# The first gate slot after two norms, computed by token tile instead of after both tiles

## The reference, cut to what matters

```python
        x = x + rms_norm(m, norm_mix_post[layer])
        f = conv_geglu_ffn(rms_norm(x, norm_ffn_pre[layer]), ffn_w_up[layer], ffn_conv_w[layer],
                           ffn_conv_b[layer], ffn_w_down[layer])
...
def conv_geglu_ffn(hn, w_up, conv_w, conv_b, w_down):
    u = depthwise_conv_centered(hn @ w_up, conv_w, conv_b)
    gate, val = jnp.split(u, 2, axis=-1)
    return (jax.nn.gelu(gate, approximate=True) * val) @ w_down
```

## Time and profile before

| | |
|---|---|
| runs | 1027.61, 1025.37, 1022.47 us |
| median | 1025.37 us |
| profiled execution, its own time | 1026.78 us |
| span from first to last instruction | 1024.9 us |
| mean granted TensorE clock (1 is 2.4 GHz) | 0.990 |
| busy: TensorE matmul / weight load | 983.2 us (96%) / 863.7 us (84%) |
| busy: VectorE / ScalarE / GpSimd | 481.9 / 623.3 / 695.9 us |

### The profile page before, as it was taken

The page is one execution under the profiler, slowest core; times in us unless marked ns, Lnnn a source line. Parts: engine busy times, 40 slices in busy tenths (PEclk is TensorE's granted clock), DMA queues, the critical chain, the costliest instruction groups (busy, mean ns, idle before and its releaser), DMA issues. The chain is left out here.

```text
span 1024.9 us, 16075 instructions
## 1 busy us (share of the span) xinstructions
PE 983.2 (96%) x6169; PEld 863.7 (84%) x6169; DVE 481.9 (47%) x993; ACT 623.3 (61%) x1145; POOL 695.9 (68%) x550
## 2 busy tenths in 40 slices
PE   6999998999999898999998899999999998999998
PEld 5898778999999797888877799999977887877786
DVE  3745344444444564777834454444353143223552
ACT  7636557555455785797867564555566568755631
POOL 5977616857577695769678657575778756866663
PEclk9999999999999999999998999999999999999999
DMA  9774325775644564745646455656455845634221
GB/s 334 252 213 156 128 81 175 236 261 170 206 165 138 164 206 126 239 139 198 206 127 222 145 187 183 203 167 205 166 164 174 205 132 180 224 124 159 88 82 42
DMA packets 131946, 178.69 MB, mean 174 GB/s; under 512 B 21457, under 2 KB 94045, under 8 KB 131677
## 3 DMA queue, kind: packets, MB, share of 16 engines
q1 hardware_dynamic: 127693, 169.95, 51.3%
q10 hardware_dynamic: 4176, 7.71, 2.3%
HBM read 176.51 MB, written 5.24 MB: 177 GB/s over the span
## 5 line engine op out<-in xcount | busy, mean ns | idle before, releaser
L519 POOL TENSOR_TENSOR wlo<-raw,whi 128x512 fp32r<-128x512 f32 (+1 forms) x514 | 673.8, 1347 | 297.6 <-ACT whi L1189 281.6
L536 PE MATMUL PS<-Th,whi 128*128 128x256 f32 (+2 forms) x1016 | 290.8, 287 | 3.5 <-DVE Tl L1715 2.8
L537 PE MATMUL PS<-Tl,whi 128*128 128x256 f32 (+2 forms) x1016 | 287.3, 283 | 0.0
L538 PE MATMUL PS<-Th,wlo 128*128 128x256 f32 (+2 forms) x1016 | 287.3, 283 | 0.0
L1189 ACT ACTIVATE whi<-raw 128x1024 fp32r<-128x1024 f32 (+1 forms) x149 | 156.0, 1047 | 165.0 <-PE PS L538 127.9
L533 PE MATMUL PS<-whi,Th 128*128 128x512 f32 (+1 forms) x512 | 204.1, 399 | 7.9 <-DVE Tl L1764 3.3
L1790 DVE SCALAR_TENSOR_TENSOR arena<-PS,cols,arena 128x255 f32<-128x255 f32 (+1 forms) x272 | 118.6, 478 | 192.1 <-ACT arena L1321 165.6
L536 PEld LDWEIGHTS PS<-Th,whi 128*128 128x128 f32 (+2 forms) x1016 | 194.9, 192 | 9.6 <-issue 5.6
L534 PE MATMUL PS<-wlo,Th 128*128 128x512 f32 (+1 forms) x512 | 198.1, 387 | 0.0
L535 PE MATMUL PS<-whi,Tl 128*128 128x512 f32 (+1 forms) x512 | 197.9, 387 | 0.0
L537 PEld LDWEIGHTS PS<-Tl,whi 128*128 128x128 f32 (+2 forms) x1016 | 194.9, 192 | 1.8 <-issue 0.7
(11 more groups left out here) (235 smaller groups left out, 1034.0 us busy)
## 6 DMA issues: line engine op xcount, KB each, us to landing
raw<-in_ffn_w_up_dram SPq DMA_DIRECT2D x44, 1024.0 KB, 5.1
raw<-in_ffn_w_down_dram SPq DMA_DIRECT2D x22, 1024.0 KB, 4.9
raw<-in_w_in_dram SPq DMA_DIRECT2D x22, 1024.0 KB, 5.1
raw<-in_c_w_in_dram SPq DMA_DIRECT2D x16, 1024.0 KB, 5.3
raw<-in_ab_w_in_dram SPq DMA_DIRECT2D x14, 1024.0 KB, 6.6
raw<-in_c_w_out_dram SPq DMA_DIRECT2D x8, 1024.0 KB, 5.8
raw<-in_ab_w_out_dram SPq DMA_DIRECT2D x4, 1024.0 KB, 4.9
raw<-in_c_w_in_dram SPq DMA_DIRECT2D x8, 512.0 KB, 5.4
```

The source lines that it names most:

```text
L519: i = nc.gpsimd.tensor_tensor(wlo[n % NLO][:, c:e], raw[n % NRAW][:, c:e], whi[n % NHI][:, c:e].bitcast(F32), ALU.subtract)
L536: mm(o, wh, ah, start=first, stop=False)
L537: mm(o, wh, al, start=False, stop=False)
L538: return mm(o, wl, ah, start=False, stop=last)
```

## The change

`norm_T` is kept for the very first norm alone, `warm` goes, and `first_gate` takes the first gate slot of both feed-forward parts. It computes the slot by token tile: 128 tokens move in place of 256, so that 96 products of 128 columns replace 48 of 256. Tile 1 is turned after 42 of the 48 products of tile 0. `post_norm` on ScalarE and VectorE takes at boundaries 1 and 3 the order that it had at boundary 4: half of the first value slot is rounded before tile 1's squares, `Th` and `Tl` of tile 0 come between the steps of tile 1, then the other half, the squares of `x`, the whole next gate slot, and `Th` of tile 1.

```diff
-            def warm(bank, n):
-
-                for _ in range(n):
-                    mm(PS[:, bank, :], ident, cst[:, 0:512], start=True, stop=True)
-
-            def norm_T(l):
...
-                    if l and t == 0:
-                        warm(4 - norm_bank(l), 3)
...
+            def first_gate(l):
+
+                s = 2 * l + 1
+                tile_T(s, 0)
+                n = slot_no[("G", l, 0)]
+                pe.wait_ge(*low(n))
+                h, w = whi[n % NHI], wlo[n % NLO]
+                for t in range(NT):
+                    for m in range(2):
+                        for k in range(KD):
+                            if (t, m, k) == (0, 1, 6):
+                                tile_T(s, 1)
+                            if m == 0:
+                                pe.wait_ge(*at("T_lo", (("n", s, t), k)))
+                            c = k * 256 + m * P
+                            i = three(PS[:, 0, m * S + t * P:m * S + (t + 1) * P], h[:, c:c + P], w[:, c:c + P],
+                                      Th[:, k, t * P:(t + 1) * P], Tl[:, k, t * P:(t + 1) * P], k == 0, k == KD - 1, False)
+                i.then_inc(*done("w_used", n))
...
-                        slot_fm(("G", l, i), 2 * (i % 2), ("n", 2 * l + 1) if i == 0 else None)
-                        if i == 0:
-                            pe.wait_ge(*at("T_lo", (("n", 2 * l + 1), KD - 1)))
+                        if i:
+                            slot_fm(("G", l, i), 2 * (i % 2))
+                        else:
+                            first_gate(l)
...
-            norm_T(1)
...
-            norm_T(3)
...
                 if l + 1 == 2:
                     high(n + 2)
-                if l + 1 == 4:
+                else:
                     high_part(n + 2, 0)
                 squares(1, 0)
                 squares(1, 1)
-                if l + 1 in (2, 4):
-                    tile_hi(0, 0, 4)
+                tile_hi(0, 0, 4)
                 root_post(1)
-                if l + 1 in (2, 4):
-                    tile_hi(0, 4)
-                    if l + 1 == 4:
-                        high_part(n + 2, 1)
-                    normed(1)
-                    high(n + 3)
-                    tile_hi(1)
-                    return
+                tile_hi(0, 4)
+                if l + 1 != 2:
+                    high_part(n + 2, 1)
                 normed(1)
-                high(n + 2)
-                T_hi(("n", l + 1), KD, 0, norm_bank(l + 1), lambda k: col(gain, k))
+                high(n + 3)
+                tile_hi(1)
```

More of the change, by code:

```diff
@@ L628, in to_T, with norm_T @@
                     i.then_inc(*done("turned", (name, k)))
-            def warm(bank, n):
-                for _ in range(n):
-                    mm(PS[:, bank, :], ident, cst[:, 0:512], start=True, stop=True)
-            def norm_T(l):
+            def norm_T():
                 for t in range(NT):
-                    if l == 0:
-                        pe.wait_ge(*at("n_hn", (l, t)))
+                    pe.wait_ge(*at("n_hn", (0, t)))
                     for k in range(KD):
-                        if l and k % 4 == 0:
-                            pe.wait_ge(*at("n_hn", (l, t, k // 4)))
-                        i = tr(PS[:, norm_bank(l) + k // 2, (k % 2) * S + t * P:(k % 2) * S + (t + 1) * P],
+                        i = tr(PS[:, norm_bank(0) + k // 2, (k % 2) * S + t * P:(k % 2) * S + (t + 1) * P],
                                hn[:, t, k * P:(k + 1) * P], ident)
                         if t == NT - 1:
-                            i.then_inc(*done("turned", (("n", l), k)))
-                    if l and t == 0:
-                        warm(4 - norm_bank(l), 3)
+                            i.then_inc(*done("turned", (("n", 0), k)))
             def tile_T(l, t):
@@ L740, in _ @@
             tr(PS[:, 0, 0:8], rowm, ident[0:8, 0:8]).then_inc(*done("mix0_T"))
-            norm_T(0)
+            norm_T()
             pe.wait_ge(*at("mix0_col"))
@@ L1740, in product @@
                     return tt(hn[:, t, 512 * hf:512 * hf + 512], PS[:, b0 + 2 * t + hf, :], gpost[:, 512 * hf:512 * hf + 512], ALU.mult)
-                tiles = l + 1 in (2, 4)
                 def post(t):
@@ L1747, in post @@
                     lk(product(t, 1))
-                    if tiles and t:
+                    if t:
                         tile_lo(0, 0, 4)
@@ L1780, in post_norm @@
                     normed(t)
[L1781 to L1784, removed]
+                tile_lo(1)
             def taps(dst, src, ws, shift):
```

## The result

The changed kernel takes **1032.58 us** (median of 20 runs, 1030.64 to 1044.58); the kernel before, on the same chips, 1025.06 (20 runs, 1022.47 to 1032.09). The ratio is **1.0089**, 95% interval 1.0070 to 1.0108: slower by 7 to 11 us. I had forecast 1028.9, with 1023.0 to 1031.9 as the range, and no change as the likeliest case. The forecast was wrong: the time lies beyond the upper end of the range, and the change is slower by more than the 0.5% that I had set as the bound. (The two medians differ by 7.5 us, the ratio of 1.0089 is 9.1; both lie in the interval.)

The account below looks back on a forecast made before the run. The prediction took TensorE, busy 96% of the span, as the bound. Later value slots, +2.4 us at boundary 1 and +1.1 at boundary 3, summed to +3.5 on 1025.37, giving 1028.9 us, range 1023.0 to 1031.9.

Parts of the forecast that it names:

- the boundary up to the wait: Boundary 1 until k = 4: boundary 4's times moved 0.48 us forward, first product at 2.75, 12 products until 4.19.
- the wait before k = 4: Tile 0's narrow products at boundary 1: TensorE waits 1.1 us for the second batch of Tl, until 5.31.
- the pitch: Step between 128-column gate products: 0.120 us taken, as the load's limit, with 0.067 as the low end.
- The second rival: Gate products: the load hides, step 0.067 us, sum -2.9, 1022.5 us; at 0.081, 1024.1 us; chance 0.15.
- the third rival: Gate products: the fixed part vanishes, step 0.107, value slot at 15.3, 1026.9 us; chance 0.65 shared with the main forecast.
- boundary 4 has the same first gap and stayed at full speed: Argument from boundary 4 against the clock falling in the new gaps at boundaries 1 and 3.
- the first rival: Boundaries 1 and 3: clock falls in the new gaps, 1.5 us each, sum 6.5, 1031.9 us; chance 0.18 with related cases.
- the clock's term: Boundaries 1 and 3: no loss in the main sum, which assumed 2.4 GHz; 1.5 us per fall otherwise.
- no wait was ended by them: Unread products before the gate: they lie inside a wait for tile 1's hn, so removing them costs nothing.
- full-clock part: Boundaries 1 and 3 at full clock: value slot at 16.3, +2.4 and +1.1, sum +3.5 us.
- clock part: Low clock for the first gate products at both boundaries: 1.5 us each, 3.0 added to the sum.

Follow-up runs that it names:

- experiment 1: Changed kernel with unread products in both new gaps, two after tile 0's turn and one before the k = 4 wait: 1025.42 us, ratio 1.0012.
- experiment 6: Changed kernel with only its first gap filled, by two unread products after tile 0's turn: 1029.28 us, ratio 1.0035.
- experiment 2: Kernel before with only the first gate slot's products made narrow, 96 of 128 columns after both tiles are turned: 1054.94 us, ratio 1.0292.
- experiment 4: Kernel before with only its unread products removed: 1025.99 us, ratio 1.0004.
- experiments 2 and 3: Kernel before with narrow gate products after both turns: 1054.94 us; the same with one more unread product behind each tile's turn: 1032.24 us.
- Experiments 7 to 10: Changed kernel with wide gate products, 1.0058; plus later roundings, 1.0045. Kernel before with two more unread products and value slot's rounding partly or wholly behind `T_hi`, 0.9987, 0.9978.

## Why the prediction was wrong, step by step

- **Right: the boundary up to the wait.** First product 2.75 (forecast 2.75), the squares of tile 1 at 0.05 and 0.81 (0.05, 0.81), the wait before k = 4 over at 5.22 (5.31), hn of tile 1 2.42 us beside GpSimd (2.46). Boundary 4 was a good source for boundary 1.
- **Nearly right: the pitch.** Forecast 0.120 out of 0.067 to 0.120, measured 0.112. That the load sets it, as the earlier trace rows said, fits: with the same 128 moving columns and 64 stationary ones it was 0.060. No experiment varied the load by itself. The 16 matmuls of the earlier trace rows are 8 fp32 products with two records each; every record has a load of its own, so 0.106 stands as the pitch of a load of 128 columns. The second rival (0.067) fell, and so did the figure of about 81 ns that the Trainium skill gives for 128-column products ("TensorE: Matmul & The Clock Gate", section "Back-to-back issue gap"): in this type and with these loads the trace has 112. With it and no loss of clock the value slot starts at 15.54 (experiment 1); the forecast 16.3 was 0.8 too late, the third rival's 15.3 was nearer.
- **Wrong: "boundary 4 has the same first gap and stayed at full speed".** This was my argument for putting the clock at nothing in the sum and giving the first rival only 0.18. The observation is correct, but behind its first product at 3.23 boundary 4 runs 18 products of 512 columns for 4.3 us before TensorE waits again, for 0.28. Here two gaps come close together with narrow products between and behind, and experiment 6 shows that filling only the first doesn't save the level.
- **Wrong: the clock's term, nothing in the sum and 1.5 us a fall in the rival.** It is the step that failed most: with a term of 0 the sum gave 3.5, and with 3.0 for two falls the range ended at 1031.9. I took the 1.5 from the earlier trace rows, where 15 wide products run low. Measured against experiment 1, with the same gate products at full clock, it is 20.14 - 15.54 = 4.6 us at boundary 1 and 18.75 - 15.54 = 3.2 at boundary 3. Three parts make boundary 1's: 35 low products, each 0.101 dearer, 3.5; the eight transposes, 1.58 instead of 0.84, 0.7; and 0.3 in the three steps behind the gap and on either side of the turn (0.27, 0.22 and 0.25 in place of 0.17, 0.12 and 0.14). The number of low products was taken from a stream of wide products that brings the clock back. The narrow one of experiment 2 didn't, and in the changed kernel it came back only behind the turn of tile 1.
- **Wrong inference: removing the unread products costs nothing, since "no wait was ended by them".** The observation is correct. What they did was to keep TensorE at work inside a wait, and that does not appear as a wait of anybody. In the kernel before they were worth 2.1 us at one boundary (experiment 4, by one timeline), and in front of narrow products two more of them decide over 9.2 (experiments 2 and 3).

The sum with measured terms: +1.6 and +0.4 for the order and the pitch, +4.6 and +3.2 for the clock, 9.8 us; measured 7 to 11. The first rival was the right mechanism, and its 1031.9 came near the measured time by luck, because two errors met: its full-clock part was too high (3.5 for 2.0) and its clock part too low (3.0 for 7.8).

**Why the early start gains nothing even at full clock.** A narrow product costs 0.112 and does one tile; a wide one costs 0.120 and does both. Before, everything behind tile 1's turn was 48 wide products, 5.8 us. Now 54 narrow ones still stand behind it, 6.0. The work done early on tile 0 is therefore not taken off the end, and tile 1's turn itself comes later (8.6 for 5.4). By the prediction's own working the value slot comes at 13.1 with a step of 0.067 and at 15.3 with 0.107; the 13.9 of boundary 1 lies between them, at a step of about 0.08 (an estimate, on a straight line). By that estimate a start 5.2 us earlier pays only below it.

**Open.** In the changed kernel the clock came back a few microseconds after tile 1's turn had begun, and in experiment 2, whose narrow stream holds no turn, it did not come back in 20 us. Whether it was the transposes that raised it was not tried by itself. Which gap is needed is half answered: the second is enough, and whether the first alone would be was not tried. Nor did I isolate what in a gap and its surroundings makes the level fall: boundary 1 fell at the second gap and boundary 3 some 1.5 us behind it, with the same instructions.

## What to carry to other kernels

Before unread products are taken out or products are cut narrower, ask what the engine will have done in each gap, and price the clock with the stream that follows the gap: wide products brought the clock back after 6 to 23, narrow ones stayed low for 94 in experiment 2 and for 35 and 22 in the changed kernel. Splitting the moving side saves nothing once the load sets the step; starting a half early pays only if the half is cheaper than the whole. And an unread product in a gap that TensorE waits through anyway is nearly free (the first gate product stood at 7.92 with two more of them and without): this made the fastest version whose gain is clear of the noise here (0.9977, 0.9965 to 0.9988).

## What was not expected of the hardware

- The same stream of 96 narrow products ran with 94 of them at 1.2 GHz or with none, by two instructions ahead of it (1.0292 against 1.0070), and TensorE had no wait inside it in either case (20 us and 11). At the low level it did not bring the clock back by itself. With a gap just before it, it could still lose the level 1.5 us in (boundary 3 of the changed kernel).
- The narrow step nearly doubles at the low clock, from 0.112 to 0.213 us, and the load's own record goes from 192 to 334 ns. A wide product goes from 0.120 to 0.21, so that at the low clock both cost the same.
- GpSimd's low parts slow two kinds of VectorE instructions that read SBUF: hn from 0.88 to 2.4 us and x from 1.41 to 2.43, each for two halves. The Trainium skill ("SBUF — State Buffer", section "Who interferes with whom") tells of such a conflict for instructions with two SBUF inputs beside a GpSimd instruction that reads SBUF, and for some forms with one. Experiments 7 to 10 agree in direction; by that rule the later one is blocked until the other ends, and no run here separates that from a mere slowing.
